# Window attention in pairs of heads: the turn of a pair one step later on TensorE, its values one step behind the turn

## The reference

```python
def ab_mixer(u, w_in, conv_w, a_log, dt_bias, a_out_g, bq_g, bk_g, sink, w_out):
    proj = u @ w_in
    qa, ka, va, za, ba, aa, qb, kb, vb = split_cols(proj, AB_SIZES)
    ya = delta_mixer(qa, ka, va, za, ba, aa, conv_w, a_log, dt_bias, a_out_g)
    ...
    yb = window_mixer(qb, kb, vb, sink)
    return jnp.concatenate([ya, yb.astype(ya.dtype)], axis=-1) @ w_out
```

```python
    s_win = jnp.einsum('bnqkgd,bnskd->bnkgqs', qb, kw).astype(jnp.float32)
    ...
    p = jax.nn.softmax(jnp.concatenate([s_win, s_meta, s_sink], axis=-1), axis=-1)
    ...
    o = (jnp.einsum('bnkgqs,bnskd->bnqkgd', p_win, vw)
         + jnp.einsum('bnkgqm,bmkd->bnqkgd', p_meta, mv))
```

## Time and profile before

| what | value |
|---|---|
| median of 3 runs | 1575.91 us (1574.42 to 1577.77) |
| the profiled execution, its own time | 1576.11 us |
| its span | 1574.3 us |
| TensorE (PE) busy | 97% of the span |
| VectorE (DVE) busy | 71% |
| ScalarE (ACT) busy | 50% |
| GpSimd (POOL) busy | 12% |
| chain that ended last | PE 85%, DVE 6%, POOL 4%, issue 2%, ACT 2%, DMA 1% |
| granted clock of TensorE, mean | 0.989 of 2.4 GHz |

### The profile page before, as it was taken

The page is one execution under the profiler, slowest core; times in us unless marked ns, Lnnn a source line. Parts: engine busy times, 40 slices in busy tenths (PEclk is TensorE's granted clock), DMA queues, the critical chain, the costliest instruction groups (busy, mean ns, idle before and its releaser), DMA issues.

```text
span 1574.3 us, 31958 instructions
## 1 busy us (share of the span) xinstructions
PE 1525.7 (97%) x12908; PEld 1475.4 (94%) x12908; DVE 1110.5 (71%) x1980; ACT 782.2 (50%) x1329; POOL 183.7 (12%) x200
## 2 busy tenths in 40 slices
PE   6997999999999999999999999999999999999997
PEld 5886899999998899999998999999999999999997
DVE  5895748776768677778777666766677666676666
ACT  4536346443455544446545555444455546554443
POOL 2592202000031100002000201000020011100000
PEclk9998999999999999999999999999999999999999
DMA  6330013444553254544534425555544444346561
GB/s 221 134 131 5 3 55 143 180 160 175 188 179 110 88 182 171 202 165 177 194 113 156 154 76 175 197 178 187 189 161 161 161 161 161 108 162 205 171 209 58
DMA packets 124790, 236.34 MB, mean 150 GB/s; under 512 B 2614, under 2 KB 50025, under 8 KB 124665
## 3 DMA queue, kind: packets, MB, share of 16 engines
q1 hardware_dynamic: 123177, 230.24, 41.6%
q0 software_dynamic: 1296, 4.28, 0.9%
q10 hardware_dynamic: 192, 0.05, 0.0%
HBM read 233.51 MB, written 1.05 MB: 149 GB/s over the span
## 4 chain that ended last, share of the span: by engine, by line
PE 85%; DVE 6%; POOL 4%; issue 2%; ACT 2%; DMA 1%; ACTq 0%; DVEq 0%; POOLq 0%
PE ps L663 48%; PE ps L710 6%; PE ps L709 6%; PE ps L708 6%; PE ps L671 5%; PE ps L832 2%; DVE w_lo L2452 2%; POOL mx L3535 2%; PE ps L809 1%; PE ps L759 1%; POOL mx L3534 1%; DVE hidden L2503 1%; PE ps L794 1%; POOL square_sum L3504 1%; PE ps L819 1%
## 5 line engine op out<-in xcount | busy, mean ns | idle before, releaser
L1730 ACT ACTIVATE w_hi<-raw 128x1024 fp32r<-128x1024 f32 x440 | 460.7, 1051 | 287.9 <-PE ps L710 135.7
L2452 DVE TENSOR_TENSOR w_lo<-raw,w_hi 128x1024 fp32r<-128x1024 f32 x440 | 547.7, 1245 | 8.3 <-ACT w_hi L1730 8.2
L663 PE MATMUL ps<-u_hi,w_hi 128*128 128x256 f32 (+1 forms) x1480 | 427.7, 289 | 3.0 <-issue 1.2
L663 PE MATMUL ps<-u_hi,w_lo 128*128 128x256 f32 (+1 forms) x1480 | 421.5, 285 | 0.0
L663 PE MATMUL ps<-u_lo,w_hi 128*128 128x256 f32 (+1 forms) x1480 | 421.0, 284 | 0.0
L663 PEld LDWEIGHTS ps<-u_hi,w_hi 128*128 128x128 f32 x1480 | 281.1, 190 | 9.5 <-issue 5.4
L663 PEld LDWEIGHTS ps<-u_hi,w_lo 128*128 128x128 f32 x1480 | 281.4, 190 | 0.0
L663 PEld LDWEIGHTS ps<-u_lo,w_hi 128*128 128x128 f32 x1480 | 280.2, 189 | 0.6
L663 PE MATMUL ps<-a_hi,w_hi 128*128 128x256 f32 x800 | 226.7, 283 | 0.6 <-DVE hidden L2503 0.3
L663 PE MATMUL ps<-a_lo,w_hi 128*128 128x256 f32 x800 | 225.0, 281 | 0.0
L663 PE MATMUL ps<-a_hi,w_lo 128*128 128x256 f32 x800 | 224.8, 281 | 0.0
(11 more groups left out here) (464 smaller groups left out, 2248.4 us busy)
## 6 DMA issues: line engine op xcount, KB each, us to landing
raw<-in_w_ff_dram SPq DMA_DIRECT2D x32, 2048.0 KB, 7.7
raw<-in_ffn_w_gu_dram SPq DMA_DIRECT2D x44, 1024.0 KB, 6.6
raw<-in_ffn_w_down_dram SPq DMA_DIRECT2D x10, 2048.0 KB, 7.8
raw<-in_xa_w_kv_dram SPq DMA_DIRECT2D x8, 2048.0 KB, 8.0
raw<-in_od_w_in_dram SPq DMA_DIRECT2D x6, 2048.0 KB, 7.9
raw<-in_w_in_ab_dram SPq DMA_DIRECT2D x5, 2048.0 KB, 7.7
raw<-in_ev_w_in_dram SPq DMA_DIRECT2D x5, 2048.0 KB, 8.0
raw<-in_xa_w_q_dram SPq DMA_DIRECT2D x4, 2048.0 KB, 8.1
```

The lines of the kernel that those rows point to most:

```text
L663: mm = pe.matmul(bank[:, 0:n], wx[:, q, k * P:(k + 1) * P], x[ux][:, k, ts], start=k == 0 and i == 0, stop=k == KD - 1 and i == 2)
L1730: act.activation(quarter(w_hi, b, q), raw_quarter(b, q), ACT.Copy).then_inc(high_split, 1)
L2452: dve.tensor_tensor(quarter(w_lo, b, q), raw_quarter(b, q), quarter(w_hi, b, q).bitcast(F32), ALU.subtract)\
```

## The change

The three loops run over one step more (k = 0 to 10). The turn of unit k moves from the end of step k to step k+1, between that step's two tiles; its copies move with it; its values, result and low part move from step k+1 to step k+2. `delta_decays` and the two `delta_sum` go behind the second tile and the turn, the copy of the sums goes to the head of VectorE's step 2, and the norms of keys and queries go from step 8 to step 9.

```diff
--- before.py
+++ after.py
@@ -1429,27 +1429,27 @@
                                        decay[0:n, c, 4 * d:4 * d + 4], start=True, stop=True)
                 mm.then_inc(M["d_cum"], 1)
 
-            for k in range(WINDOW_UNITS + 1):
+            for k in range(WINDOW_UNITS + 2):
                 if k < WINDOW_UNITS:
                     window_scores(k)
                 if k < 7:
                     qkvz_tile(2 * k + 2)
                 if k == 0:
                     pe.wait_ge(M["ab_turn_read"], 1)
+                if k >= 2:
+                    window_values(k - 2)
+                if k == 2:
+                    pe.wait_ge(M["d_cum_read"], 1)
+                if 1 <= k <= WINDOW_UNITS:
+                    window_turn(k - 1)
+                if k < 7:
+                    qkvz_tile(2 * k + 3)
                 if k == 1:
                     pe.wait_ge(at_copied, 1)
                     delta_decays()
                 if k == 8:
                     delta_sum(KEYS)
-                if k >= 1:
-                    window_values(k - 1)
-                if k < 7:
-                    qkvz_tile(2 * k + 3)
-                if k == 1:
-                    pe.wait_ge(M["d_cum_read"], 1)
-                if k < WINDOW_UNITS:
-                    window_turn(k)
-                if k == 8:
+                if k == 9:
                     delta_sum(QUERIES)
             for i, (m, source) in enumerate(turn_list):
                 delta_turn(i, m, source)
@@ -2087,19 +2087,19 @@
                     act.wait_ge(M["d_cum_read"], 1)
                     act.activation(necc[0:NMETA, 0], gcc[0:NMETA, 0], ACT.Exp)
                     act.activation(necc[:, 1:3], gcc[:, 1:3], ACT.Exp).then_inc(M["d_gate_exp"], 1)
-                if k == 8:
+                if k == 9:
                     delta_logs(KEYS)
-                if k >= 1:
-                    window_result(k - 1)
+                if k >= 2:
+                    window_result(k - 2)
                 if k < 6:
                     next_split(2 * k + 3)
                 if k == 7:
                     act.wait_ge(M["silu_done"], 1)
                     for which in (KEYS, QUERIES):
                         act.activation(delta_sq[which], delta_heads[which], ACT.Square).then_inc(M["d_sq"], 1)
-                if k < WINDOW_UNITS:
-                    window_copies(k)
-                if k == 8:
+                if 1 <= k <= WINDOW_UNITS:
+                    window_copies(k - 1)
+                if k == 9:
                     delta_logs(QUERIES)
             for i, (m, source) in enumerate(delta_turns()):
                 n = TILES[m][1] - TILES[m][0]
@@ -2907,28 +2907,28 @@
                     .then_inc(M["d_normed"], 1)
 
             dve.wait_ge(M["sink_meta"], 1)
-            for k in range(WINDOW_UNITS + 1):
+            for k in range(WINDOW_UNITS + 2):
+                if k == 2:
+                    dve.wait_ge(M["d_cum"], 1)
+                    dve.tensor_copy(gcc[0:NMETA, 0], tile_bank[3][0:NMETA, 0:8])
+                    dve.tensor_copy(gcc[:, 1:3], tile_bank[3][:, 8:24].rearrange("p (c h) -> p c h", c=2)).then_inc(M["d_cum_read"], 1)
                 if k < WINDOW_UNITS:
                     window_logits(k)
                 if k < 8:
                     qkvz_step(2 * k + 1)
                 if k < WINDOW_UNITS:
                     window_normalise(k)
-                if k == 1:
-                    dve.wait_ge(M["d_cum"], 1)
-                    dve.tensor_copy(gcc[0:NMETA, 0], tile_bank[3][0:NMETA, 0:8])
-                    dve.tensor_copy(gcc[:, 1:3], tile_bank[3][:, 8:24].rearrange("p (c h) -> p c h", c=2)).then_inc(M["d_cum_read"], 1)
                 if k < 7:
                     qkvz_step(2 * k + 2)
-                if k == 8:
+                if k == 9:
                     delta_norm(KEYS)
-                if k >= 1:
-                    window_low(k - 1)
+                if k >= 2:
+                    window_low(k - 2)
                 if k == 0:
                     delta_gates()
                 if k in CONV_DVE:
                     conv(CONV_DVE[k])
-                if k == 8:
+                if k == 9:
                     delta_norm(QUERIES)
             dve.wait_ge(M["d_cum_read"], 1)
 
```

## The result

| | before | changed |
|---|---|---|
| median us, 7 runs each | 1577.12 (1574.42 to 1580.14) | 1582.97 (1580.84 to 1583.82) |
| ratio to before | | 1.0033, 95% interval 1.0018 to 1.0047 |
| span of the profiled execution, us | 1574.3 | 1581.2 |
| its mean granted clock | 0.989 | 0.984 |

The account below looks back on a forecast made before the run. GpSimd was taken to bound the stage up to the SiLU, the attention's unit-by-unit latency behind it. Terms 0 + 0 + 3.3 = +3.3 us gave 1579.2 us, range 1575.2 to 1582.6.

Parts of the forecast that it names:

- the main term: Behind the SiLU: one more round before the sum of the keys' squares, which starts 3.3 us later.
- The walk: Behind the SiLU: instructions stepped forward at present durations and clock; keys' sum starts at 135.8 us instead of 132.44.
- The head at no cost: Before the SiLU: GpSimd sets the end, and VectorE's delay of about 0.7 us is covered; taken 0.
- The cover of 1.48: At the SiLU: ScalarE's exponents of unit 6 and table load have 1.48 us in hand.
- rival C: Before the SiLU: copy of the sums delays VectorE by 2.7 us, SiLU 1.2 late: 1580.4 us; chance 0.14.
- the prices of the forecast: GpSimd's convolutions before the SiLU: one meeting with VectorE more or fewer would be 0.9 us.
- as long as VectorE is not earlier: Before the SiLU: eleven low parts stay in GpSimd's stretch, unless VectorE is earlier or over 3 us later; taken 0.
- the term of the clock: Behind the SiLU: keys' sum at the low clock as before, the clock's return shifted by about 3.3 us; no extra cost.
- rival D: Behind the SiLU: low clock lasts through the queries' sum, 1580.5 to 1582.8 us; chance 0.14.
- Rival A: Behind the SiLU: unbroken TensorE work brings the full clock before about 133 us; no change, 1575.9 us; chance 0.19.
- Rival B: Before the SiLU: TensorE's waits were on the path, SiLU up to 4.0 us earlier, 1571.9 us; chance 0.08.

Follow-up runs that it names:

- Tail alone: Against the kernel before: old order and old place of the copy of the sums up to unit 3, changed order from unit 4 on; ratio 1.0040.
- head, caught up: Changed order up to step 6, copies of unit 0 ahead of unit 1's exponents, old order resumed before the SiLU; 1.0007 of the kernel before.
- early copies: The changed kernel with only the copies of unit 0 moved ahead of the exponents of unit 1 on ScalarE; 1.0044 of the kernel before.
- fill, changed: The changed kernel with eight matmuls of unused result on TensorE beside the SiLU; 1.0033 of the kernel before.
- head alone: Against the kernel before: changed order for units 0 to 2 and the copy of the sums, two units in step 3, old order behind; 1.0052.
- fill, before: The kernel before with eight matmuls of unused result on TensorE beside the SiLU; ratio 1.0011.
- before again: The kernel before, unchanged, timed and profiled a second time; ratio 1.0000.
- the three fill runs with eight matmuls: Eight unused matmuls beside the SiLU in the kernel before, the changed kernel, and the changed kernel with copies ahead of squares; 1.0011, 1.0033, 1.0018.
- the run with six: The kernel before with work of units 5 to 8 moved earlier around the SiLU, plus six unused matmuls behind the scores of unit 8; 0.9995.
- changed kernel again: The changed kernel itself, timed and profiled a second time; 1.0041 of the kernel before.
- units during the SiLU: The kernel before with unit 5's result ahead of the SiLU, unit 8's scores and logits earlier, unit 6's copies and unit 8's exponents heading step 7; 1.0016.

## Why the prediction was right or wrong

**Direction, and the main term: right.** The forecast put the loss behind the SiLU, in one round more. The walk gave 135.8 for the start of the keys' sum; it was 136.01, less 0.3, 135.7. Values of unit 5 at 126.57 came at 126.87, the wait of some 1 us for the copies behind the squares was 0.96. Tail alone has the loss without the head and the caught-up head is back at 15.09 us, so this is shown. Across the changed kernel (twice), tail alone, early copies and fill, changed the sum starts 3.27 to 3.28 us later behind the SiLU than before, against 3.3 in the forecast; at its end the round is worth 2.8 to 3.2, because the clock rose within some of the sums.

**The head at no cost: right, for less margin than said.** The decays took 2.06 us, not 1.24 to 1.9, since TensorE's low clock covered all of them. VectorE was 1.5 us late at once, the end of the range of 0.9 to 1.5, and it carried 1.4 to step 6 where I wrote 0.7: I had half of it made up by the reading of tile 6 and gave no reason, for an engine that is saturated from there on. The cover of 1.48 was used up to the last 0.05 us, and the SiLU started 66.49 and 66.52 us behind L2841 in the two executions, against 66.51 before, so rival C is refuted.

The start of the SiLU takes one of two values in the table, 66.36 to 66.52 us or 67.44 to 67.48 (head alone apart), 0.95 us and so, by the prices of the forecast, one meeting of VectorE and GpSimd apart. Before has 66.51, and with fill, whose head is the same instruction for instruction, 67.46. What differs is where VectorE's low parts stand. VectorE in before, then with fill; and the same stretch of TensorE in before, then with fill:

```profile
77.54 1.62 DVE L2452 TENSOR_TENSOR w_lo<-raw,w_hi 128x1024 fp32r<-128x1024 f32 x1
```

```profile
76.91 1.52 DVE L2456 TENSOR_TENSOR w_lo<-raw,w_hi 128x1024 fp32r<-128x1024 f32 x1
```

```profile
72.00:80.00 8.00, 6.85 (x29) 0.57 0.55 195
```

```profile
72.00:80.00 8.00, 6.89 (x53) 1.00 0.56 185
```

This low part starts 22.7 us behind L2841 in before and 22.1 with fill, where the clock had not fallen beside it. In the four executions with the late SiLU it starts at 22.1, in the other nine at 22.5 to 24.2. So GpSimd ends later where VectorE is earlier, be it by the order or by the clock, which stayed full beside this low part in fill, before and in tail alone. The forecast's condition, "as long as VectorE is not earlier", and its price of 0.9 fit this; that an added meeting is the reason is argued from the starts and was not tested. The Trainium skill ("SBUF — State Buffer", who interferes with whom) has issue order decide which side blocks. The one pair of rows read for it agrees: GpSimd's L3534 that started at 118.22, behind VectorE's L2452 of 117.71, took 1.50 us instead of 0.64.

**The step that was mis-sized is the term of the clock.** "The walk has the new sum at the low level too, with the return shifted by about the same 3.3 us" entered the sum as 0. Of the 4.5 and 4.3 us by which the two profiled executions of the changed kernel are late at the delta rule, the round is 3.27 and 3.28, so the clock took 1.3 and 1.0 us more than in the first profile of before, and 2.0 and 1.7 more than in before again. In one execution it stayed low through the queries' sum (3.51 us instead of 2.00). In the other it came back within the keys' sum and fell once more ahead of L1419. The first is the mechanism of rival D, the second is not, and in no other kernel with the changed order did the queries' sum run at the low clock (2.10 us in all five). Rival D put 4.6 to 6.9 us over the kernel before; that the measured 5.2 and 6.5 us (0.0041 x 1577) lie there is in part luck. The forecast of 3.3 lies within the interval of the first measurement (2.8 to 7.4) and under that of the second (3.9 to 9.0).

I kept to "shifted" because the clock's fall was already in the trace; what I didn't price was that the return differs from one execution to the next. The Trainium skill ("TensorE: Matmul & The Clock Gate", why this matters for your kernels) advises against idle gaps between bursts; the prediction cited it and gave it 0 in the sum. The runs agree in part. With waits of 1.4 to 2.8 us the clock fell in the three fill runs with eight matmuls, while with one of 1.50 us it stayed up in the run with six (up to 150 us). But in the eight executions with 9.3 us it fell near the end of the stage with no wait over 0.7 us since it had come back.

**Rival A** (an early return, no change) is refuted: TensorE worked from 126.87 to 131.07 without a pause and stayed at 1.2 GHz. Even with the full clock in this place (fill, changed) the round didn't get shorter, because the copies behind the squares bound it. **Rival B** is refuted: TensorE's waits grew from 4.0 us to one of 6.1 and the SiLU started as before, so they are off the path.

**What stays open.** The trace of the changed kernel is 6.9 us longer than the first of before: 4.8 at the delta rule, 3.6 at 400 us, and 3.2 more with the stretches at 0.79 near 460 and 508 us. The changed kernel again has neither stretch; it is 4.2 us late at the delta rule and 4.5 at the end, with a span of 1578.9, 4.6 over the first of before and 8.0 over before again. Measured times are another matter: all five timings of kernels whose sum starts 3.27 us late (changed twice, tail alone, early copies, fill changed) are 5.2 to 6.9 us over before by their ratios, so about 2 to 3.6 us stand beyond the round (of which the later SiLU of tail alone and early copies is 0.95). The clock up to the delta rule gives 1.0 to 1.3 of that in the changed kernel's traces, but the head, caught up, loses 1.5 to the same late fall and measures only 1.0007; the rest has no cause shown. Over the table, late at the delta rule and the measured ratio go together: four kernels late by 2.2 to 3.2 us measure 1.0007 to 1.0019, and five late by 4.3 to 5.6 measure 1.0033 to 1.0052; fill, changed (3.3 and 1.0033) and the two with units during the SiLU (-0.2 and -3.7, for 1.0016 and 0.9995) don't fit it well. Whether a late stage also makes low stretches further on more likely, or whether those are chance, was not settled. Neither was why the clock fell ahead of L1419 in eight executions of the table and not in the other six, before twice among them.

## What to carry to other kernels

Deepening a software pipeline by a step moves work across whatever barrier stands in it. Count the rounds that have to run behind that barrier (here the SiLU, which GpSimd sets) before counting the waits that go; a wait on an engine that isn't the limit is worth nothing, and a round behind the limit is worth its full latency. Where a stage runs at half clock, price the return of the clock as a term of its own, with both ends, and read it from two profiles of the same kernel. Measure a round up to the start of what waits for it, not to its end, so that the clock does not enter. Filling a pause with idle matmuls kept the clock up through the stage in one of four runs, and no gain in time was shown.

## What the runs showed of the hardware

- **A run's time goes with its mean granted clock.** Over 95 timed executions of the kernel before beside the other runs (1572.3 us at 0.994 to 1584.64 at 0.982), a straight line gives about 0.96 us for 0.001 of mean clock (correlation -0.83). The changed kernel's seven runs have 0.984 to 0.987. A profile of before with 0.989 and one with 0.994 differ by 3.4 us of span, from the same instructions. This is why 0.2% of this kernel takes 12 runs and more to see, and why a profile is to be compared with a second profile of the same kernel first.
- **The low clock outlasts unbroken work.** In the changed kernel TensorE worked without a pause from 126.87 to 131.07 us, from 132.03 to 135.1 and from 136.01 on, and the granted clock stayed 0.50 until near 145. In the other execution, with the same waits up to the keys' sum, it was back near 138.6.
- **It also falls in short waits.** In before with fill it was 1.00 up to 130 us and 0.52 from there to 137, around a wait of 2.44 us.
- **It falls with hardly a wait, too.** In the changed kernel again it went from 1.00 to 0.50 between 145 and 146 us, while TensorE worked without a pause from 143.68 on (L1389, then L1419), behind a wait of 0.66 us. In before the same matmuls behind a wait of 0.61 us ran at 1.00.
